# Third block's convolution branch for 128 tokens ahead of the gathers, its other 384 tokens behind them

## What is computed

```python
h = modulate(rmsnorm(x, norm1_g), sh1, sc1)
gate_b, gate_c, xa, xr, gr = split(h @ w_in)           # five times 512 columns
y_a = gate_b * causal_dwconv(gate_c * xa, conv_a_w)    # kernel of 3
xr  = causal_dwconv(xr, conv_b_w) + conv_b_b           # kernel of 4
y_b = rg_lru(xr, ...) * gelu(gr)
y   = concat(head_rmsnorm(y_a), head_rmsnorm(y_b)) @ w_out
x   = x + g1 * y
h   = modulate(rmsnorm(x, norm2_g), sh2, sc2)
x   = x + g2 * peer(h, w_q, sub_keys, expert_u, expert_v)
return rmsnorm(x, final_g)
```

## Time and profile before

| | |
|---|---|
| median of the runs | 1756.47 us (1756.17 to 1756.67) |
| profiled execution | 1756.17 us |
| its span, first to last instruction | 1754.1 us |
| PE, DVE, ACT, POOL busy | 1559.4, 1378.4, 811.3, 752.9 us |
| granted TensorE clock, mean | 0.991 |
| bytes by DMA | 620.68 MB, mean 354 GB/s |

### The profile page before, as it was taken

The page is one execution under the profiler, slowest core; times in us unless marked ns, Lnnn a source line. Parts: engine busy times, 40 slices in busy tenths (PEclk is TensorE's granted clock), DMA queues, the critical chain, the costliest instruction groups (busy, mean ns, idle before and its releaser), DMA issues.

```text
span 1754.1 us, 21411 instructions
## 1 busy us (share of the span) xinstructions
PE 1559.4 (89%) x4862; PEld 828.0 (47%) x4862; DVE 1378.4 (79%) x3037; ACT 811.3 (46%) x2093; POOL 752.9 (43%) x554
## 2 busy tenths in 40 slices
PE   9999999999999998998788888888888887988887
PEld 6888888788644443433333333333333333333332
DVE  5788987688898888778787777877777877777777
ACT  5233333555345445344635445354535445454535
POOL 2000000000255545555566656456665655566662
PEclk9999999999999999999999999999999999999999
DMA  6565572242699999999999999999999999999998
GB/s 241 192 218 202 182 286 96 79 180 85 265 418 421 421 421 422 421 421 421 409 422 422 421 422 421 422 422 422 422 422 422 422 422 422 422 422 422 422 422 338
DMA packets 93294, 620.68 MB, mean 354 GB/s; under 512 B 11440, under 2 KB 11456, under 8 KB 23872
## 3 DMA queue, kind: packets, MB, share of 16 engines
q0 software_dynamic: 77936, 566.81, 78.3%
q1 hardware_dynamic: 15168, 53.00, 8.3%
q10 hardware_dynamic: 144, 0.26, 0.0%
HBM read 617.94 MB, written 2.10 MB: 353 GB/s over the span
## 4 chain that ended last, share of the span: by engine, by line
PE 36%; DMA 33%; issue 9%; DVE 7%; POOL 5%; DVEq 4%; ACT 4%; ACTq 1%; POOLq 0%; SPq 0%
DMA arena<-in_experts,idx 32%; PE ps L797 10%; PE ps L502 7%; PE ps L503 7%; PE ps L504 7%; POOL arena L491 5%; DVE arena L1785 3%; DVEq L1600 2%; PE ps L681 1%; ACTq L1122 1%; ACT arena L1125 1%; ACT stats L1123 1%; DVEq L1731 1%; ACT lnw L1121 1%; DVEq L1640 1%
## 5 line engine op out<-in xcount | busy, mean ns | idle before, releaser
L797 PE MATMUL ps<-arena 128*128 128x512 f32 x2048 | 985.6, 615 | 181.7 <-ACT arena L1125 172.6
L491 POOL DMA_INDIRECT arena<-in_experts,idx x512 | 729.6, 1425 | 678.9 <-PE ps L797 348.7
L1785 DVE CUSTOM_DVE_ANT_0 arena<-arena 128x1024 f32<-128x1024 f32 x512 | 626.2, 1224 | 183.1 <-DMA arena<-in_experts,idx 173.3
L797 PEld LDWEIGHTS ps<-arena 128*128 128x128 f32 x2048 | 363.4, 191 | 754.7 <-ACT arena L1125 446.3
L1121 ACT ACTIVATE lnw<-lnw 128x1 f32<-128x1 f32 x512 | 103.8, 203 | 581.1 <-DVE lnw L1785 575.9
L1125 ACT ACTIVATE arena<-ident,stats 128x128 f32<-128x128 f32 x512 | 205.5, 401 | 35.3
L1123 ACT ACTIVATE stats<-lnw 128x1 f32<-128x1 f32 x512 | 150.8, 295 | 35.2
L454 POOL DMA_DIRECT2D arena<-in_w_ada x24 | 12.8, 535 | 213.7 <-DVE ada L1258 213.7
L1121 ACT ACT_TABLE_LOAD x64 | 82.1, 1283 | 7.2 <-issue 6.3
L1258 DVE SCALAR_TENSOR_TENSOR ada<-arena,cact,ada 128x512 f32<-128x512 f32 x96 | 72.2, 752 | 16.9 <-DMA arena<-in_w_ada 9.7
L1219 DVE TENSOR_TENSOR w_hl<-arena,w_hl 128x1024 fp32r<-128x1024 f32 x44 | 53.7, 1221 | 24.4 <-ACT w_hl L852 24.4
(11 more groups left out here) (321 smaller groups left out, 1793.1 us busy)
## 6 DMA issues: line engine op xcount, KB each, us to landing
arena<-in_w_ada POOLq DMA_DIRECT2D x24, 1024.0 KB, 5.4
arena<-in_w_in SPq DMA_DIRECT2D x43, 512.0 KB, 3.4
arena<-in_w_out SPq DMA_DIRECT2D x22, 512.0 KB, 4.5
arena<-in_experts,idx POOLq DMA_INDIRECT x512
lnw<-in_w_in SPq DMA_DIRECT2D x8, 512.0 KB, 3.9
arena<-in_w_grp POOLq DMA_DIRECT2D x4, 1024.0 KB, 7.8
arena<-in_w_q SPq DMA_DIRECT2D x1, 3072.0 KB, 13.1
xres<-in_x SPq DMA_DIRECT2D x4, 512.0 KB, 11.8
```

The lines of the kernel that those rows point to most:

```text
L491: nc.gpsimd.indirect_dma_start(slot(n), None, experts, bass.IndirectOffsetOnAxis(ap=idx[:, e, n:n + 1], axis=0)).then_inc(arr[n % RING], 16)
L797: last = mm(ps[half][:, :], lhsT=diag[:, n % RING, :], rhs=slot(n)[:, DM + half * T:DM + (half + 1) * T], start=(e == 0 and n == 0), stop= ...
L1785: nc.vector.tensor_tensor_reduce(out=urow, in0=urow, in1=rows, scale=1.0, scalar=0.0, op0=ALU.mult, op1=ALU.add, accum_out=dots[:, e, n:n ...
```

## The change

- The third block (j = 2, `LAST - 1`) is treated as the last one was. Its chunks GCT, XA and GB (indices `RAW` = 12, 13, 14) are no longer split; they are loaded raw into a new place `extra` (12 KB a partition) without waiting for the ring of split chunks, and multiplied as plain f32 with `h1_first`, for 128 tokens. VectorE's and ScalarE's operations of that branch run over 128 columns, and the third block's `head_means(5)` is a plain product over 128 columns. The ring goes on with the last block's XR and GR, so these are loaded and split one turn sooner.
- The last block's `w_last` chunks are loaded when the ring is done with chunks 10 and 11, no longer after 14 and 15.
- For the other 384 tokens the three chunks are loaded once more (`w_rest`, into the places of W_q's heads 5 to 7). TensorE does their 24 products (`rest_mm`, one k each) at positions 5 to 15, 17 to 27 and 33 to 43 behind the gathers. W_q's heads 5, 6 and 7 are loaded one at a time, when each of the three is done.
- A second set of `rest_piece`, `rest_square`, `rest_root` and a copy `rest_copy` runs at positions 30 to 58. The W_out2 products of the later tiles are respread over positions 29 to 166, so some are now in the second tile; the `h2_piece` positions of the other tiles move from 47 to 157 to 72 to 188, and the comparisons on VectorE and ScalarE cover 6 turns for 5. `late_root(2, 3)` comes 32 positions later.
- TensorE's loop over the tiles 1 to 3 is unrolled. The wait for the last W_out2 sums to be read stands before the transposes of the next tile and not before the loop.

```diff
+LATER_ORDER = (0, 1, 4, 5, 6, 7, 3, 2)
-LATE = dict(zip((*range(5, 48, 2), *range(50, 78, 3), *range(92, 123, 2)), ...
-LATE_PAIRS = 5
-DVE_SLOT, ACT_SLOT = 34, 55
+GCT2_AT = (5, 6, 8, 9, 11, 12, 14, 15)
+XA2_AT = (17, 18, 20, 21, 23, 24, 26, 27)
+GB2_AT = (33, 34, 36, 37, 39, 40, 42, 43)
+LATE = dict(zip((29, 31, *range(44, 51, 2), *range(52, 64, 2), 65, 66, 67, 69, *range(74, 120, 3), *range(121, 168, 3)), ...
+LATE_PAIRS = 6
+DVE_SLOT, ACT_SLOT = 38, 59
+RAW = range(5 * LAST - 3, 5 * LAST)
+SPLITS = [i for i in range(NSPLIT) if i not in RAW]
-REST_MEAN = 24
+REST_COPY = 30
+REST_SQUARE = (22, 48)
+REST_MEAN = (24, 50)
+REST_ROOT = (25, 54)
...
+        extra = sb("extra", [P, 12 * KB])
-        h1_rest = view(40, KD * REST).rearrange("p (k t) -> p k t", k=KD)
+        h1_rest = extra[:, :].rearrange("p (k t) -> p k t", k=KD)
+        w_rest = {GCT: view(20, DM), XA: view(24, DM), GB: view(28, DM)}
...
-                elif n >= FIRST2 + WSLOTS:
-                    sp.wait_ge(w_mm, mm_count(n - WSLOTS))
+                elif n >= FIRST2 + WSLOTS and n - FIRST2 not in RAW:
+                    sp.wait_ge(w_mm, mm_count(ring_of(n) - WSLOTS))
...
-            for s, after in ((GB, 5 * LAST - 1), (GCT, 5 * LAST), (XA, 5 * LAST)):
+            for s, after in ((GB, RAW[0] - 2), (GCT, RAW[0] - 1), (XA, RAW[0] - 1)):
...
+            load_wq(0, 0, 2)
+            load_wq(1, 2, 5)
+            for s in (GCT, XA, GB):
+                sp.dma_start(w_rest[s], w_in2[LAST - 1, s, :, :]).then_inc(rest_in[s], 16)
+            for n in range(3):
+                sp.wait_ge(w_mm, NSEQ + 5 * NJ + 4 + n)
+                load_wq(2 + n, 5 + n, 6 + n)
...
-                if n // 2 == LAST:
+                if n // 2 == LAST or n == 2 * LAST - 1:
...
+                    if n - FIRST2 in RAW:
+                        pe.wait_ge(*raw_arrival(n))
+                        pe.wait_ge(h1_whole, 1)
+                        pe.wait_ge(read_by[s], j)
+                        last_mm(s, h1_first, range(KD), w=raw_of(n))
+                        continue
...
-            pe.sem_inc(slot_free, 1)
+            pe.sem_inc(slot_free, 2)
...
+            def rest_mm(s, k):
+                if k == 0:
+                    pe.wait_ge(rest_in[s], 16)
+                    pe.wait_ge(*{GCT: (y2_read, 1), XA: (gc_copied, NJ + 1), GB: (gc_copied, NJ + 2)}[s])
+                last_mm(s, h1_rest, range(k, k + 1), w_rest[s], REST_BANK[1][s])
...
-            with pe.Fori(1, NT, 1) as t:
+            for t in range(1, NT):
...
-                ca = slice(0, P if j == LAST else T)
+                ca = slice(0, P if j >= LAST - 1 else T)
...
-                n = P if j == LAST else T
+                n = P if j >= LAST - 1 else T
...
-            late_rows = {55: 1, 85: 2, 129: 3}
-            late_roots = {56: (1, 1)}
+            late_rows = {78: 1, 124: 2, 175: 3}
+            late_roots = {79: (1, 1)}
...
-            late_rest = {16: 0, 17: 1, 18: 2, 19: 3, 20: 4, 28: 5, 29: 6}
+            late_rest = {16: (0, 0), 17: (0, 1), 18: (0, 2), 19: (0, 3), 20: (0, 4), 28: (0, 5), 29: (0, 6),
+                         34: (1, 0), 35: (1, 1), 36: (1, 2), 37: (1, 3), 47: (1, 4), 57: (1, 5), 58: (1, 6)}
...
-    nc = bacc.Bacc("TRN2", target_bir_lowering=False, num_devices=1)
+    nc = bacc.Bacc("TRN2", target_bir_lowering=False, num_devices=1, dynamic_dma_scratch_size=4096)
```

More of the change, by code:

```diff
@@ L66 @@
 STEPS = NT * HEADS
-REST_MEAN = 24
+REST_COPY = 30
+REST_SQUARE = (22, 48)
+REST_MEAN = (24, 50)
+REST_ROOT = (25, 54)
+REST_BANK = ({GCT: GCT, XA: XA, GB: GB}, {GCT: 5, XA: GCT, GB: 5})
 SLOTS = HEADS * TOPK
@@ L190, in mixers_and_peer @@
         hot8 = ada[:, 0, 256:384].rearrange("p (k c a) -> p k c a", k=EIGHT, c=2)
-        h2next = junk2 = ada[:, 4, :]
+        h2next = junk2 = extra[:, 2 * DM:]
         coef = stats[:, 4:6]
@@ L213, in raw_of @@
                 return view((76 + 8 * i if i < 4 else 60 + 8 * (i - 4)) + 4, DM)
-            r = n % WSLOTS
+            if n - FIRST2 in RAW:
+                i = n - FIRST2 - RAW[0]
+                return extra[:, i * DM:(i + 1) * DM]
+            r = ring_of(n) % WSLOTS
             if r < WSLOTS - 1:
@@ L224, in raw_arrival, with split_count @@
                 return res_arr[n - NSEQ], 16
-            return raw2_arr[n % WSLOTS], 16 * ((n - FIRST2) // WSLOTS + 1)
+            if n - FIRST2 in RAW:
+                return raw3_arr[n - FIRST2 - RAW[0]], 16
+            return raw2_arr[ring_of(n) % WSLOTS], 16 * ((ring_of(n) - FIRST2) // WSLOTS + 1)
+        def split_count(n):
+            return n - sum(FIRST2 + r <= n for r in RAW)
         def mm_count(n):
@@ L262, in mixers_and_peer @@
         raw2_arr = [sem(f"raw2_arr{r}") for r in range(WSLOTS)]
+        raw3_arr = [sem(f"raw3_arr{i}") for i in range(len(RAW))]
         res_arr = [sem(f"res_arr{r}") for r in range(NRES)]
@@ L271, in mixers_and_peer @@
         bd_in, keys_in, wout2_in, fing_in = map(sem, ("bd_in", "keys_in", "wout2_in", "fing_in"))
-        wq_in = [sem(f"wq_in{i}") for i in range(2)]
+        wq_in = [sem(f"wq_in{i}") for i in range(5)]
+        rest_in = {s: sem(f"rest_in{s}") for s in (GCT, XA, GB)}
         consts = sem("consts")
@@ L806, in expert_step @@
                         pe.wait_ge(score_ready, 2 * HEADS * t + 2 * h)
+                        if t == 0 and 5 <= h < HEADS:
+                            pe.wait_ge(wq_in[h - 3], 16)
                         query(h, query_out(h))
@@ L816, in expert_step @@
                         pe.wait_ge(h2n_ready, t)
+                        pe.wait_ge(y2_read, 4)
                         transpose_h2(h2next, 2)
[L818 to L824, removed]
+                    at = SLOTS * t + TOPK * e + n
+                    for s, when in ((GCT, GCT2_AT), (XA, XA2_AT), (GB, GB2_AT)):
+                        if at in when:
+                            rest_mm(s, when.index(at))
+                    if at in LATE:
+                        product = LATE[at]
                         if product == (1, 1, 0):
                             pe.wait_ge(v_ready, NJ + 1)
+                            pe.wait_ge(yT_ready, 2 * NJ + 1)
+                        if product == (1, 0, 0):
+                            pe.wait_ge(v_ready, NJ + 2)
                         if product == (1, 0, 6):
                             pe.wait_ge(yT_ready, 2 * NJ + 2)
+                        if product == (1, 0, 7):
+                            pe.wait_ge(yT_ready, 2 * NJ + 3)
+                        if product == (2, 1, 0):
+                            pe.wait_ge(ya_ready, NJ + 2)
                         if product == (2, 0, 0):
-                            pe.wait_ge(rn_ready, 2 * NJ + 2)
+                            pe.wait_ge(rn_ready, 2 * NJ + 3)
                         if product == (3, 0, 0):
@@ L833, in expert_step @@
                         wout2_mm(*product)
-                    if later and TOPK * e + n == REST_MEAN:
-                        pe.wait_ge(sq_ready, 2 * NJ + 1)
+                    if at in REST_MEAN:
+                        r = REST_MEAN.index(at)
+                        pe.wait_ge(sq_ready, 2 * NJ + 1 + r)
+                        pe.wait_ge(rn_ready, 2 * NJ + 1 + r)
                         mm(ps[4][:, 0:REST], lhsT=headmean, rhs=sqa1, start=True, stop=True).then_inc(norm_mm, 1)
```

132 lines of the change are left out of this document (72 added, 60 removed).

## The result

The changed kernel takes 1758.51 us (median of 22 runs, 1756.88 to 1760.21), the kernel before 1755.93 beside it on the same chip (22 runs, 1754.78 to 1757.16): a ratio of 1.0016, interval 1.0010 to 1.0022, or 2.6 us more. I had said 1753.3, with 1755.4 as the upper end. The profiled execution has a span of 1756.2 and a time of 1757.99, against 1754.1 and 1756.17.

A forecast was written before the change was run, and what follows sets the result against it. TensorE was taken to bound the lead and DMA the gather stage. Lead -5.4, bytes +3.35 and boundary hole -1.0 sum to -3.05 us: 1753.1 from the profiled time 1756.17, stated as 1753.3, range 1751.0 to 1755.4.

The forecast's parts named there:

- the sum of -3.05: Whole kernel: lead -5.4, second weight reading +3.35, tile boundary -1.0 us, against the profiled span of 1754.1.
- TensorE's unrolled tiles ... cost nothing, since each of these engines waits for a gather in every step: Gather stage: unrolled tiles, moved buffers, extra loop comparisons and split semaphores were put at no cost.
- The cover I named: Gather stage: gathers already in flight hide engine stalls; a 6.87 us Pool wait at 1166 still left 421 GB/s.
- a chain ... that doesn't start earlier: Lead: VectorE's and ScalarE's work behind the third block's gates starts at 409.22 as before, so head_means(4) can start at 417.2.
- Standstill and clock: Lead: TensorE idles 4.1 us before the head means, then a lower clock costs 1.7; 7.1 us gained becomes 5.4.
- The rival in which the clock holds: Lead: no clock fall after TensorE's idle, so lead -7.1, total -4.75, time 1751.7; chance 0.21.
- Bytes: Behind the gathers: three chunks read again, 1.573 MB at 421 GB/s, cost 3.7 us, taken as 3.35.
- The hole at 500 to 510: First tile: a 405 GB/s stretch, 0.4 us short, takes up part of the bytes read again.
- The hole at the boundary: Before 856.62: moving late_root(2, 3) 32 positions later wins back 1.0 of 1.3 us; bounds 0 and 1.3.
- Scratch, slots, ring in the first tile: Gather stage: smaller descriptor scratch costs nothing, and TensorE keeps pace with the gathers, so no new hole.
- the rival of the dry ring: First tile: new products make TensorE late and gathers go missing; all 5.5 us would give +2.5, 1759.0; chance 0.06.
- that of the capped gathers: Gather stage: smaller scratch limits gathers in flight, deciding below about 3; a cap of one costs hundreds of us; chance 0.02.

The follow-up runs named there:

- the load-order run: Changed kernel with chunk 15 loaded ahead of the three raw chunks 12 to 14 and chunk 16 behind them: 1758.87 us, ratio 1.0016 to the kernel before.
- the order alone: Changed kernel with the last block's head_means(4) and (5) moved from behind chunk XR to behind chunk GR: 1753.18 us, ratio 0.9982 to the kernel before.
- the table run: Changed kernel with a tiny Gelu on ScalarE ahead of the third block's gelu_gate, loading the table before the wait: 1757.23 us, ratio 1.0006 to the kernel before.
- the scratch run: Kernel before with only the descriptor scratch made smaller (4096 bytes): 1756.21 us, ratio 1.0003.
- the run with 32 never executed products: Changed kernel with 32 small products, never executed, placed behind TensorE's last tile: 1758.12 us, ratio 1.0010 to the kernel before.

## Why the prediction was wrong

Against the sum of -3.05, the span went up by 2.1. The 5.15 between them are 2.7 in the lead, 2.4 in the gather stage and 0.1 at the end.

- **"TensorE's unrolled tiles ... cost nothing, since each of these engines waits for a gather in every step": this is the step that failed.** Alone, on the kernel before, it costs 2.4 us. The cover I named hides TensorE's time, not the bytes of its program on a DMA with none to spare (0.17 MB, 0.4 us), nor a start of the whole program that is 1.2 us later. The Trainium skill ("Runtime: NRT & Kernel Launch", Instruction fetch mechanics) has the crossing of an instruction block as mostly hidden and full unrolling as what kernels prefer where possible; by it this edit is free, and the run doesn't agree (2.4 us, ratio 1.0013). The profiled executions with tiles 1 to 3 in one or two loops have 6.6 to 7.1 us of holes in the gather stage (6 of them), those with all written out 7.2 to 8.5 (10). Part of it lies at the third tile boundary: in 1485 to 1515 the first six have 0.1 us of hole at most, eight of the other ten 0.3 to 1.3. That is shown as a difference; its mechanism isn't. Putting tiles 2 and 3 of the new form back in a loop returned 0.6 us of the stage once and 1.3 once, and nothing of the late start. What the start owes to the written-out tiles is not shown, only that it was late in all ten executions that have them (16.1 to 17.3) and in the two with a loop for tiles 2 and 3 (16.7, 16.9), against 15.6 to 16.05 in the four others.
- **"a chain ... that doesn't start earlier"** was right, but it starts later: VectorE's first operation at 411.95 instead of 409.22 is the start's 1.2, the Gelu table's 1.28 and 0.25 that I can't place. I had counted the splits that leave ScalarE as a gain of idle time and not looked at which instruction then stands behind the wait.
- **Standstill and clock:** the place was right, and the length (4.67 for 4.1) within what the table adds. The third block's gates, which I took as unmoved, came 2.1 us later: the start's 1.2 and, by the load-order run, 0.9 from the order of the loads. In after's profiled execution the clock's price is 1.7 us, as in the sum: 0.1 of it in 410 to 420 and 1.6 in 420 to 430. But the size was not a constant, see below: 3.4 us in six of the eight executions with this standstill. The rival in which the clock holds happened in none of them.
- **Bytes:** 1.573 MB / 421 = 3.7 was right by the bytes moved, and by the medians of the run without them (4.1, within the noise of two medians; its one profiled stage shows 2.8). The hole at 500 to 510 did fill.
- **The hole at the boundary:** 1.0 was to come back. By stretches of 5 us, the shortfall around 850 is 1.4 us before and 1.0 after (1.6 to 1.9 in the three other kernels with before's executed work, so between 0.4 and 0.9 came back). Holes at later boundaries took 0.3 of it (1400 to 1540). The wait shrank to 6.97 us as forecast and a hole stayed, so the length of the wait alone doesn't tell the hole.
- **Scratch, slots, ring in the first tile:** as predicted. The first 40 us of gathers have holes of 2.8 us against 2.7, so neither the rival of the dry ring nor that of the capped gathers played a part. In the dry ring's sum the W_out2 products up to position 69 are 16, so it is 29.8 us and not 30.4, 4.8 more and not 5.5; nothing hangs on it. The loss came from the side where I had put 0 without bounds, and from the chain's late start.

## What to carry to other kernels

Work taken off the busiest engine in a lead is worth only what the next chain leaves of it: move something into the gap in the same edit (the order alone was worth 5.3 us here), and look again at what now stands right behind each wait, table loads above all. Where the DMA is full, the bytes of a program are on the bill (0.4 us here for 0.17 MB), and more than the bytes was lost, so write loops out only as far as the work differs. And an edit priced at nothing "because the engine waits anyway" should be given a bound from running it alone, since it reaches the start of the program and the DMA as well.

## What the runs showed of the hardware

The price of TensorE's fall to 1.2 GHz came in two sizes. Summed as (1 - granted clock) x length, every standstill of the lead (3.3 to 5.4 us long) and every one at a tile boundary came with 1.7 us or with 3.4 us of lost full-speed work, with nothing between, and the same kernel's boundaries differ: the kernel before lost 3.4, 1.7 and 3.4. In the lead, after and the table run lost 1.7; six others with the same standstill 3.4, among them the load-order run, whose rows are

```profile
410.00:420.00 10.00, 4.63 (x19) 3.53 (x19) 7.00 (x15) 5.21 (x9) 0.00 (x0) 0.91 0.00 0
420.00:430.00 10.00, 10.00 (x32) 7.44 (x31) 7.34 (x7) 1.56 (x3) 0.00 (x0) 0.75 0.00 1
```

Where it was 1.7 at the first boundary, kernels of the new form had 0.1 to 0.3 us of hole there (3 executions), where it was 3.4 they had 0.6 to 1.5 (8). Kernels with the same executed work got different sizes at the same place (before and the scratch run, after and the run with 32 never executed products), so what decides it is not shown. It is wide enough to hide a gain such as an earlier start: the kernel with 32 never executed products started 0.7 us ahead of after, lost 3.4 instead of 1.7 (1.1 of it inside the standstill, where it costs nothing: 417.11 to 419.23 has a clock of 0.50 and no busy TensorE), and had its first gather at the same 459.6.
